# Time mix of a model on one core: the recurrence joined with the output stage, the state's decay on GpSimd, the head statistics on ScalarE by chunk, the bonus during the inversion

## The chip, the cores and the metric

The kernel runs on one core of one Trainium2 chip. Its time is the device time of one execution in microseconds (us). A core has TensorE (matmuls), VectorE, ScalarE, GpSimd (elementwise work) and SyncE, which here only issues loads. In the profile they are PE, with PEld for its weight loads, DVE, ACT, POOL and SP.

## The reference, cut to what matters

The model has two blocks over 256 tokens of width 1024. The second has two layers: feed-forward, mixer, feed-forward. The mixer of the last layer is `rwkv7_time_mix`, with 16 heads of 64. Its end is what the change touches:

```python
def step(state, inp):
    r_t, d_t, k_t, v_t, kk_t, a_t = inp
    sa = einsum('bhij,bhj->bhi', state, -kk_t)
    state = (state * d_t[:, :, None, :] + sa[..., None] * (kk_t * a_t)[:, :, None, :]
             + v_t[..., None] * k_t[:, :, None, :])
    return state, einsum('bhij,bhj->bhi', state, r_t)
_, y = lax.scan(step, zeros, xs)                        # the recurrence
mean = jnp.mean(y, -1, keepdims=True)                   # over the 64 of a head
var = jnp.mean(jnp.square(y - mean), -1, keepdims=True)
y = ((y - mean) * lax.rsqrt(var + RWKV_GN_EPS)).reshape(b, s, d)
y = y * ln_g + ln_b
bonus = jnp.sum(r_ * k_ * r_k, -1, keepdims=True) * v_
y = y + bonus.reshape(b, s, d)
return (y * g) @ w_o                                    # g = sigmoid(xg @ g1) @ g2, g1 1024x160, g2 160x1024
```

## The kernel before, in words

The time mix is four stages, each a block: all engines begin a block together, and the next begins when all are through. They are `rwkv_factors`, `rwkv_inverse`, `rwkv_chunks` and `rwkv_output`; `project_joined` with `w_o` follows, then the feed-forward. Inside a block each engine works through its own list in the order written, and waits on semaphores (`wait_ge`) that others raise (`then_inc`). `link(engine, signal, instruction)` makes the engine wait for the end of its own instruction.

The 256 tokens are 8 chunks of 32 (`N_RC`, `RC`). A tile of y for one chunk is 128 partitions by 256: partition 32q + t is token t of quarter q, and the four quarters hold four heads of 64 each. A matmul of 32 output columns takes one of four column tiles of TensorE's array (`tile_position=(0, 32q)`); a loop over q inside fills the four. The shape of the tile, rows * columns, stands in the profile's rows as 128*32, 32*32, 64*32 or 32*64, and each matmul call in float32 is two records there.

- `rwkv_inverse` makes the 32x32 products of each chunk and head (L3482), inverts the triangles on VectorE (L3571, L3572), makes the values `v` (L3467, copied at L3539), the bonus factors `bon` (L3500) and what the chunks add (`nv`, `kv`). VectorE is through some time before the end of the block, and GpSimd has nothing.
- `rwkv_chunks` goes through the chunks in order. TensorE reads the state S (L3603), VectorE adds (L3646, `W`), TensorE multiplies with the inverse (L3616), VectorE and ScalarE copy one half each (L3652, L3638), TensorE makes the state's update (L3625) and the chunk's y (L3630), VectorE adds them to the decayed state (L3661) and to y (L3655, L3666). The decay of the old state, `Sd = S * cl + kv`, is two VectorE operations of 128x512 (L3648, L3649) in chunks 1 to 6, between L3646 and the copy L3652.
- `rwkv_output` is one pass at full width, 128x2048. VectorE: sum over heads (L3733), mean (L3734), centring (L3735), sum of squares (L3737), reciprocal (L3739), scaling (L3740), gain (L3742), plus bonus and shift (L3744), times the gate (L3746). ScalarE: squares (L3717) and root (L3719). GpSimd: bonus times values (L3724) plus shift (L3727), into `g`. TensorE: the gate g2 in two parts, first all 32 calls with rows 0 to 127 (`ga`, L3704), then all 32 with rows 128 to 159 (`gb`, L3709), each with q inside.
- `project_joined` transposes y (L3195), rounds the weights (L2923) and multiplies (L2898 to L2900).

Weights come through 8 slots of 1 MB. SyncE's `advance` (L401) loads the next unit of a fixed order when the unit in its slot is freed, and its waits stand in that order.

## Time and profile before

| | us |
|---|---|
| time, median of 3 runs | 1957.58 (1957.23 to 1958.78) |
| time of the profiled execution | 1958.1 |
| its span in the trace | 1956.3 |
| inversion to the end, about | 1600 to 1662 |
| recurrence, about | 1662 to 1698.4 |
| output stage, about | 1698.4 to 1719.2 |

Times inside the trace are counted from the start of the span. A row of the order of time is start and duration in us, engine, line, operation, output<-inputs, shapes, how many instructions are merged, and in brackets how long the engine had been idle and what released it. The ends of matmuls are modelled. `PEclk` is the granted clock of TensorE, as a share of 2.4 GHz; 0.50 is 1.2 GHz.

### The profile page before, as it was taken

The page shows a single profiled execution, that of the slowest core. Times are in us where ns is not written, and L with a number is a line of the kernel's source. Part 1 is how long each engine was busy: PE and PEld are TensorE (multiplying, and loading weights), DVE is VectorE, ACT ScalarE, POOL GpSimd, SP SyncE. Part 2 cuts the span into 40 slices and gives each one's busy share as a digit, 9 for nine tenths or more (in the row PEclk, how much of TensorE's full clock was granted, in tenths as well). Part 3 has the DMA queues.
Part 4 walks back from the last instruction along what each step waited for, and adds up shares of the span by engine and source line. Part 5 has one row for each costly group of instructions (what it writes and reads, how often), then busy time and mean ns, then how long its engine had stood idle before and what let it go on. Part 6 is the DMA issues. An engine that isn't in the chain of part 4 may idle for free. (4 is left out here: it accounts for less than half of the span.)

```text
span 1956.3 us, 30051 instructions
## 1 busy us (share of the span) xinstructions
PE 1758.5 (90%) x12670; PEld 1304.8 (67%) x12670; DVE 1105.6 (57%) x1993; ACT 655.7 (34%) x1037; POOL 10.4 (1%) x6
## 2 busy tenths in 40 slices
PE   6898789988988899999987999999998988769998
PEld 5343256763323588888875788878886876558887
DVE  4332254452322777773578677677777372658665
ACT  3111013331100644442243544464444302045443
POOL 0000000000000000000000000000000000200000
PEclk9898889989987999999978999999999989779999
DMA  8999972279999755434211455545542312045540
GB/s 357 415 421 421 421 293 80 93 298 420 421 421 421 296 194 193 162 104 183 105 47 58 157 178 188 183 162 189 180 168 84 131 38 89 4 150 189 182 168 22
DMA packets 58190, 405.27 MB, mean 207 GB/s; under 512 B 6416, under 2 KB 7824, under 8 KB 10432
## 3 DMA queue, kind: packets, MB, share of 16 engines
q1 hardware_dynamic: 58048, 403.25, 53.5%
q8 instruction: 104, 1.70, 0.4%
q14 instruction: 38, 0.31, 0.0%
HBM read 402.18 MB, written 1.05 MB: 206 GB/s over the span
## 5 line engine op out<-in xcount | busy, mean ns | idle before, releaser
L2092 PE MATMUL ps<-ffn_x,ffn_wh 128*128 128x512 f32 x1408 | 496.2, 407 | 10.4 <-DVE ffn_x L2226 7.2
L2095 PE MATMUL ps<-ffn_x,ffn_wl 128*128 128x256 f32 x1408 | 376.6, 281 | 0.0
L2092 PEld LDWEIGHTS ps<-ffn_x,ffn_wh 128*128 128x128 f32 x1408 | 269.6, 192 | 84.1 <-issue 11.0
L2233 DVE TENSOR_TENSOR ffn_wl<-w,ffn_wh 128x2048 fp32r<-128x2048 f32 x132 | 301.4, 2286 | 1.7 <-ACT ffn_wh L2177 0.3
L2095 PEld LDWEIGHTS ps<-ffn_x,ffn_wl 128*128 128x128 f32 x1408 | 258.2, 189 | 1.6
L2177 ACT CAST ffn_wh<-w 128x2048 fp32r<-128x2048 f32 (+1 forms) x140 | 252.9, 1806 | 4.5 <-PEq L715 3.5
L2192 ACT COPY ffn_part_low<-ps 128x512 f32<-128x512 f32 x88 | 51.5, 585 | 338.7 <-PE ps L2095 337.9
L2237 DVE TENSOR_TENSOR ffn_z<-ps,ffn_part_low 128x512 f32<-128x512 f32 x88 | 60.8, 690 | 161.2 <-ACT ffn_part_low L2192 161.0
L2136 PE MATMUL ps<-ffn_wh,ffn_hidh 128*128 128x512 f32 x352 | 138.2, 393 | 0.4 <-issue 0.4
L2138 PE MATMUL ps<-ffn_wh,ffn_hidl 128*128 128x512 f32 x352 | 137.5, 391 | 0.0
L2137 PE MATMUL ps<-ffn_wl,ffn_hidh 128*128 128x512 f32 x352 | 137.3, 390 | 0.0
L1196 DVE TENSOR_TENSOR slot_y<-ps,slot_y 128x512 fp32r<-128x512 f32 x32 | 22.1, 691 | 124.5 <-ACT slot_y L1148 124.5
L1148 ACT CAST slot_y<-ps 128x512 fp32r<-128x512 f32 x32 | 18.7, 586 | 187.6 <-PE ps L1053 187.6
L1236 DVE TENSOR_TENSOR h<-h,ps 128x272 f32<-128x272 f32 x128 | 50.9, 434 | 53.9 <-PE ps L1066 53.8
L1028 PE MATMUL ps<-w,xg 128*32 128x512 f32 x560 | 75.7, 635 | 4.2 <-DMA w<-in_moe_gu 4.2
L2136 PEld LDWEIGHTS ps<-ffn_wh,ffn_hidh 128*128 128x128 f32 x352 | 66.1, 188 | 15.1 <-issue 0.7
L2138 PEld LDWEIGHTS ps<-ffn_wh,ffn_hidl 128*128 128x128 f32 x352 | 66.1, 188 | 14.7
L2137 PEld LDWEIGHTS ps<-ffn_wl,ffn_hidh 128*128 128x128 f32 x352 | 66.1, 188 | 12.7
L1028 PE MATMUL ps<-w_extra,xg 128*32 128x512 f32 x416 | 59.2, 670 | 4.0 <-DMA w_extra<-in_moe_gu 4.0
L2241 DVE TENSOR_TENSOR ffn_z<-ffn_z,rs 128x512 f32<-128x512 f32 x88 | 60.5, 691 | 2.9
L1065 PE MATMUL ps<-spread,slot_y 128*128 128x272 f32 x128 | 46.6, 381 | 12.5 <-DVE h L1236 8.3
L1053 PE MATMUL ps<-w_extra,slot_hidT 128*32 128x512 f32 x256 | 39.8, 732 | 11.8 <-DMA w_extra<-in_moe_dn 10.8
(588 smaller groups left out, 2722.0 us busy)
## 6 DMA issues: line engine op xcount, KB each, us to landing
w<-in_ffn_gu SPq DMA_DIRECT2D x88, 1024.0 KB, 4.8
w<-in_moe_gu SPq DMA_DIRECT2D x70, 1024.0 KB, 18.6
w_extra<-in_moe_gu SPq DMA_DIRECT2D x52, 1024.0 KB, 25.9
w<-in_ffn_dn SPq DMA_DIRECT2D x44, 1024.0 KB, 4.8
w_extra<-in_moe_dn SPq DMA_DIRECT2D x32, 1024.0 KB, 26.2
w<-in_moe_dn SPq DMA_DIRECT2D x26, 1024.0 KB, 26.8
sq<-in_moe_dn SPq DMA_DIRECT2D x6, 1024.0 KB, 27.9
sq<-in_moe_gu SPq DMA_DIRECT2D x6, 1024.0 KB, 26.5
```

What stands on the lines that cost most here:

```text
L1028: mm = nc.tensor.matmul(K.ps[R, i % 2, :], xg[:, i % 2, k, R], w[:, j * 512:(j + 1) * 512], start=k == 0, stop=k == KT - 1, tile_position= ...
L1236: v.tensor_tensor(K.h[:, m], K.h[:, m], K.ps[:, 6 + m % 2, 0:L1], ALU.add).then_inc(added.sem, 1)
L2092: return nc.tensor.matmul(pair_of(b)[:, a], high[:, s, tile(a, k)], X[:, k], start=k == 0, stop=False)
L2095: return nc.tensor.matmul(pair_of(b)[:, a, 0:SEQ], low[:, s, tile(a, k)], XH[:, k], start=False, stop=k == KT - 1)
L2136: nc.tensor.matmul(out, hidh[:, f, tok], high[:, s, w], start=first, stop=False)
L2137: nc.tensor.matmul(out, hidh[:, f, tok], low[:, s, w], start=False, stop=False)
L2138: mm = nc.tensor.matmul(out, hidl[:, f, tok], high[:, s, w], start=False, stop=final)
L2177: nc.scalar.copy(high[:, n % parts, at], S.buf(units[n])[:, at]).then_inc(*w_high.one())
L2192: nc.scalar.copy(part_low[:], pair_of(b)[:, :, SEQ:]).then_inc(*low_copied.one())
L2233: nc.vector.tensor_tensor(low[:, s], S.buf(units[n]), high[:, s], ALU.subtract).then_inc(*w_split.one())
L2237: nc.vector.tensor_tensor(z[:, b % 2], pair_of(b)[:, :, 0:SEQ], part_low[:], ALU.add).then_inc(*added.one())
L2241: nc.vector.tensor_tensor(z[:, b % 2], z[:, b % 2], K.rs[:, 1:2, 0:SEQ].to_broadcast([P, 2, SEQ]), ALU.mult).then_inc(*scaled.one())
```

## The change

`rwkv_output` is gone. Its work goes to three places.

- **Inversion.** GpSimd makes bonus and shift in `g`, as soon as the last values are copied.
- **Recurrence.** GpSimd makes `Sd` in chunks 1 to 6, behind the state's update. VectorE sums the heads of chunk c-1 (`total`) ahead of its copy, and subtracts the mean of chunk c-2 (`centre`) behind it. ScalarE scales the sum to the mean and squares chunk c-1 head by head, with the sum in the accumulator (`spread`).
- **End, in the same block.** `root`, reciprocal, scaling, gain, bonus are done for two halves of four chunks, and the gate multiplies two chunks at a time. TensorE makes the gate after its last chunk by `gate(c)`, in other banks and columns of PSUM.

The core of the diff:

```diff
+ in rwkv_inverse:
+        @block.gpsimd
+        def _(pool):
+            pool.wait_ge(*v_taken.at(N_RC))
+            by = bon[:].rearrange("p c (h a) -> p (c h) a", a=1).to_broadcast([P, 4 * N_RC, HD])
+            link(pool, bonus_made, nc.gpsimd.tensor_tensor(heads(g[:]), heads(v[:]), by, ALU.mult))
+            pool.wait_ge(*S.arrived(unit))
+            nc.gpsimd.tensor_tensor(g[:], g[:], ln[:, 1:2].to_broadcast([P, N_RC, QW]), ALU.add)
+ in rwkv_chunks, SyncE:
+            S_.advance(sp)
+ TensorE:
+            def gate(c):
+                tok = slice(c * RC, (c + 1) * RC)
+                for q in range(4):
+                    R, cols = quad(q), slice(q * QW, (q + 1) * QW)
+                    nc.tensor.matmul(K.ps[R, (c + 4) % 8, QW:2 * QW], low[:, 0, tok], S_.buf(ga)[:, cols], start=True, stop=False, tile_position=(0, q * RC))
+                    mm = nc.tensor.matmul(K.ps[R, (c + 4) % 8, QW:2 * QW], low[0:GATE_LORA - P, 1, tok], S_.buf(gb)[:, cols], start=False, stop=True,
+                                          tile_position=(0, q * RC))
+                if c % 2:
+                    mm.then_inc(*g_made.one())
...
+            pe.wait_ge(*S_.arrived(ga))
+            pe.wait_ge(*S_.arrived(gb))
+            for c in range(N_RC):
+                if c == 4:
+                    pe.wait_ge(*y_done.at(N_RC))
+                gate(c)
+ ScalarE:
+            def spread(c):
+                act.wait_ge(*sum_made.at(c + 1))
+                link(act, K.act_step, nc.scalar.activation(st[:, 1, c], st[:, 0, c], ACT.Copy, scale=-1.0 / HD))
+                for h in range(4):
+                    last = nc.scalar.activation(junk[:], y[:, c, h * HD:(h + 1) * HD], ACT.Square, bias=st[:, 1, c, h], accum_out=st[:, 2, c, h])
+                    if h < 3:
+                        link(act, K.act_step, last)
+                last.then_inc(*spread_made.one())
+            def root(i):
+                act.wait_ge(*spread_made.at(N_RC // 2 * (i + 1)))
+                nc.scalar.activation(st[:, 3, halves[i]], st[:, 2, halves[i]], ACT.Sqrt, bias=K.eps[:, 2:3], scale=1.0 / HD).then_inc(*rooted.one())
             for c in range(N_RC):
                 act.wait_ge(*sa_made.at(2 * c + 2))
                 nc.scalar.copy(SA[:, P:2 * P], K.ps[:, 3, 0:P]).then_inc(*sa_ready_a.one())
+                if c:
+                    if c > 1:
+                        act.wait_ge(*spread_made.at(c - 1))
+                    spread(c - 1)
+            root(0)
+            act.wait_ge(*spread_made.at(N_RC - 1))
+            spread(N_RC - 1)
+            root(1)
+        @block.gpsimd
+        def _(pool):
+            for c in range(1, N_RC - 1):
+                pool.wait_ge(*st_ready.at(c))
+                link(pool, carried, nc.gpsimd.tensor_tensor(Sd[:], S[:], cl[:, :, c:c + 1].to_broadcast([P, KT, HD]), ALU.mult))
+                nc.gpsimd.tensor_tensor(Sd[:], Sd[:], kv[c], ALU.add).then_inc(*carried.one())
+ VectorE:
+            def total(c):
+                dve.wait_ge(*y_done.at(c + 1))
+                vv.reduce_sum(st[:, 0, c], heads(y[:, c]), AX).then_inc(*sum_made.one())
+            def centre(c):
+                dve.wait_ge(*spread_made.at(c + 1))
+                at = heads(y[:, c])
+                vv.tensor_tensor(at, at, st[:, 1, c].to_broadcast([P, 4, HD]), ALU.add).then_inc(*centred.one())
             for c in range(N_RC):
                 if c:
                     dve.wait_ge(*as_made.at(c))
                     vv.tensor_tensor(of_g(W), of_par[:, :, :, 0], of_g(nv[0][:, c]), ALU.add).then_inc(*w_ready.one())
-                    if c < N_RC - 1:
-                        link(dve, K.dve_step, vv.tensor_tensor(Sd[:], S[:], cl[:, :, c:c + 1].to_broadcast([P, KT, HD]), ALU.mult))
-                        vv.tensor_tensor(Sd[:], Sd[:], kv[c], ALU.add).then_inc(*K.dve_step.one())
-                        carried = K.dve_step.now()
+                    total(c - 1)
                 dve.wait_ge(*sa_made.at(2 * c + 1))
                 vv.tensor_copy(SA[:, 0:P], K.ps[:, 2, 0:P]).then_inc(*sa_ready.one())
+                if c > 1:
+                    centre(c - 2)
...
                     if c:
-                        dve.wait_ge(*carried)
+                        dve.wait_ge(*carried.at(2 * c))
...
+            total(N_RC - 1)
+            for i, part in enumerate(halves):
+                n = N_RC // 2
+                dve.wait_ge(*rooted.at(i + 1))
+                link(dve, K.dve_step, vv.reciprocal(st[:, 4, part], st[:, 3, part]))
+                for c in (N_RC - 2, N_RC - 1) if i else ():
+                    centre(c)
+                dve.wait_ge(*centred.at(n * (i + 1)))
+                at = heads(y[:, part].rearrange("p c n -> p (c n)"))
+                by = st[:, 4, part].rearrange("p c h a -> p (c h) a").to_broadcast([P, 4 * n, HD])
+                link(dve, K.dve_step, vv.tensor_tensor(at, at, by, ALU.mult))
+                link(dve, scaled, vv.tensor_tensor(y[:, part], y[:, part], ln[:, 0:1].to_broadcast([P, n, QW]), ALU.mult))
+                link(dve, K.dve_step, vv.tensor_tensor(y[:, part], y[:, part], g[:, part], ALU.add))
+            for p in range(4):
+                dve.wait_ge(*g_made.at(p + 1))
+                pair, banks = slice(2 * p, 2 * p + 2), slice((2 * p + 4) % 8, (2 * p + 4) % 8 + 2)
+                vv.tensor_tensor(y[:, pair], y[:, pair], K.ps[:, banks, QW:2 * QW], ALU.mult)
```

## Rows read from the trace of the kernel before

**Rows 1.** The page, engine totals: busy us, share of the span, instructions.

```profile
PE 1758.5 (90%) x12670; PEld 1304.8 (67%) x12670; DVE 1105.6 (57%) x1993; ACT 655.7 (34%) x1037; POOL 10.4 (1%) x6
```

**Rows 2.** Windows: recurrence, gate products by clock, output stage, projection's start.

```profile
core 0: us, PE busy (x) PEld busy (x) DVE busy (x) ACT busy (x) POOL busy (x), PEclk, DMA share, GB/s
1662.00:1698.40 36.40, 27.54 (x1184) 21.14 (x1184) 23.23 (x49) 2.12 (x8) 0.00 (x0) 0.69 0.02 5
1698.40:1702.60 4.20, 3.77 (x37) 2.02 (x41) 3.85 (x3) 0.00 (x0) 3.71 (x2) 0.51 0.00 0
1702.60:1707.90 5.30, 5.28 (x96) 2.70 (x88) 3.32 (x2) 1.91 (x1) 5.30 (x1) 1.00 0.02 3
1698.40:1719.20 20.80, 9.05 (x128) 4.72 (x128) 17.77 (x9) 2.23 (x2) 10.24 (x2) 0.66 0.18 66
1727.40:1733.10 5.70, 5.64 (x13) 4.46 (x14) 0.01 (x1) 0.06 (x1) 0.00 (x0) 0.50 0.51 185
```

**Rows 3.** Order of time, output stage: start, duration, engine, line, idle before.

```profile
1697.95 0.42 DVE L3666 TENSOR_TENSOR rw_r<-ps,rw_r 128x256 f32<-128x256 f32 x1 [0.54 <-PE ps L3630]
1701.00 1.40 DVE L3734 TENSOR_SCALAR rw_st<-rw_st 128x32 f32<-128x32 f32 x1
1716.74 2.29 DVE L3746 TENSOR_TENSOR rw_r<-rw_r,ps 128x2048 f32<-128x2048 f32 x1
1719.33 3.65 PE L3195 MATMUL ps<-cst,rw_r 128*128 128x128 f32 x16 [11.45 <-PEq L3673]
```

**Rows 4.** Order of time, TensorE: end of the recurrence and both gate products.

```profile
1696.81 1.07 PE L3630 MATMUL ps<-rw_a,rw_sc 32*32 32x64 f32 x32
1698.83 5.47 PE L3704 MATMUL ps<-w,rw_low 128*32 128x256 f32 x64 [0.94 <-PEq L3581]
1704.22 3.65 PE L3709 MATMUL ps<-w,rw_low 32*32 32x256 f32 x64
```

**Rows 5.** Order of time, TensorE: two lines of one shape, then two shapes.

```profile
1606.73 2.47 PE L3493 MATMUL ps<-cst,rw_kk 128*32 128x128 f32 x84
1609.02 0.85 PE L3500 MATMUL ps<-cst,rw_r 128*32 128x2 f32 x77
...
1674.42 0.68 PE L3625 MATMUL ps<-rw_a,rw_bp 32*64 32x64 f32 x32 [0.46 <-DVE rw_a L3652]
1675.03 0.65 PE L3630 MATMUL ps<-rw_a,rw_sc 32*32 32x64 f32 x32
```

**Rows 6.** Full-array matmuls by line; then L3704's durations, ns min/median/max.

```profile
L3267 PE MATMUL ps<-rw_mix,w 128*128 128x256 f32 (+1 forms) x160 | 34.9, 380 | 0.0
...
L3704 PE MATMUL ps<-w,rw_low x64: 379/577/635, 1698.8 to 1703.9; 128*32 128x256 f32 x64
```

**Rows 7.** One chunk in order of time; then L3625 by line.

```profile
1672.41 0.42 DVE L3646 TENSOR_TENSOR rw_a<-ps,xn 128x256 f32<-128x256 f32 x1
1673.64 0.27 ACT L3638 COPY rw_a<-ps 128x128 f32<-128x128 f32 x1 [3.88 <-PE ps L3616]
1674.08 0.28 DVE L3652 COPY rw_a<-ps 128x128 f32<-128x128 f32 x1
1675.24 0.69 DVE L3661 TENSOR_TENSOR rw_sg<-ps,rw_sg 128x512 f32<-128x512 f32 x1 [0.55 <-PE ps L3625]
...
1679.45 0.69 DVE L3661 TENSOR_TENSOR rw_sg<-ps,rw_sg 128x512 f32<-128x512 f32 x1 [0.41 <-PE ps L3625]
...
L3625 PE MATMUL ps<-rw_a,rw_bp 32*64 32x64 f32 x224 | 5.1, 294 | 2.1 <-DVE rw_a L3652 1.4 <-ACT rw_a L3638 0.5 <-issue 0.2
```

**Rows 8.** Order of time, GpSimd.

```profile
1698.74 3.62 POOL L3724 TENSOR_TENSOR rw_g<-rw_v,rw_bonus 128x2048 f32<-128x2048 f32 x1 [1698.30 <-POOLq L3581]
1702.50 6.63 POOL L3727 TENSOR_TENSOR rw_g<-rw_g,w 128x2048 f32<-128x2048 f32 x1
```

**Rows 9.** By line and shape, ScalarE: activation with a bias tile, accumulator read.

```profile
L2736 ACT ACTIVATE nsa_p<-nsa_s,nsa_stat 128x128 f32<-128x128 f32 x16 | 6.4, 402 | 39.9 <-DVE nsa_stat L2848 39.9
...
L2736 ACT ACTIVATION_READ_ACCUMULATOR nsa_p<-nsa_s,nsa_stat 128x1 f32 x32 | 6.0, 186 | 0.0
```

More of the change, by code:

```diff
@@ L3185, in rwkv @@
             kv = [x.rearrange("p (f i) -> p f i", i=HD) for x in kv]
-            rwkv_inverse(K, a, k, r, kk, ar, bp, kp, sc, bon, mix_v, v, kv, tm, nv, flat(sg), flat(K.xn))
+            ln_unit = rwkv_inverse(K, a, k, r, kk, ar, bp, kp, sc, bon, mix_v, v, kv, tm, nv, flat(sg), flat(K.xn), g)
             tm = tm.rearrange("p (t u) -> p u t", t=RC)
-            rwkv_chunks(K, ar, cl, bp, kv, sc, tm, nv, y, flat(a), flat(sg))
-            rwkv_output(K, y, v, low, g, bon, flat(K.xn)[:, 0:2 * D])
+            K.retire("kv_made", "kv_taken", "out_turned")
+            rwkv_chunks(K, ar, cl, bp, kv, sc, tm, nv, y, flat(a), flat(sg), low, g, ln_unit)
         def turn(m):
@@ L3427, in _, with rwkv_inverse @@
             receptance(7)
-def rwkv_inverse(K, bt, kt, rk, kend, ar, bp, kp, sc, bon, mix_v, v, kv, turned, nv, room, room2):
+def rwkv_inverse(K, bt, kt, rk, kend, ar, bp, kp, sc, bon, mix_v, v, kv, turned, nv, room, room2, g):
     nc, S = K.nc, K.stream
@@ L3438, in rwkv_inverse @@
         made, masked, ends_made, ends_taken = K.sig("tile_made"), K.sig("tile_stored"), K.sig("t_made"), K.sig("taken_a")
-        bonus_made, inverted = K.sig("out_made"), K.sig("taken_v")
+        rk_made, inverted = K.sig("out_made"), K.sig("taken_v")
         v_made, v_taken, v_unit = K.sig("lin_made"), K.sig("lin_stored_s"), K.sig("unit_done")
@@ L3445, in rwkv_inverse @@
             S.free(wv[j], v_unit.at(j + 1) if j < 3 else v_made.at(N_RC))
+        unit, bonus_made = S.take("ln_rows"), K.sig("scaled")
+        ln = S.buf(unit).rearrange("p (j n) -> p j n", j=2)
+        heads = lambda ap: ap.rearrange("p c (h d) -> p (c h) d", d=HD)
         tok = lambda c: slice(c * RC, (c + 1) * RC)
@@ L3501, in _ @@
                                           tile_position=(0, f % 4 * RC))
-            mm.then_inc(*bonus_made.one())
+            mm.then_inc(*rk_made.one())
             pe.wait_ge(*ends_taken.at(8))
@@ L3534, in _ @@
                 nc.scalar.copy((bp, kp)[n // 4][:, 2 * (n % 4):2 * (n % 4) + 2], K.ps[:, n].rearrange("p (s n) -> p s n", s=2)).then_inc(*ends_taken.one())
-            act.wait_ge(*bonus_made.at(1))
+            act.wait_ge(*rk_made.at(1))
             nc.scalar.copy(bon[:], K.ps[:, 0, 0:4 * N_RC].rearrange("p (c h) -> p c h", c=N_RC))
@@ L3574, in _, with rwkv_chunks @@
             vv.transpose(square(turned), T[:]).then_inc(*inverted.one())
-def rwkv_chunks(K, ar, cl, bp, kv, sc, tm, nv, y, room, room2):
-    nc = K.nc
-    with ExitStack() as ctx:
+        @block.gpsimd
[5 more added lines that the diff above has]
+            nc.gpsimd.tensor_tensor(g[:], g[:], ln[:, 1:2].to_broadcast([P, N_RC, QW]), ALU.add)
+    return unit
+def rwkv_chunks(K, ar, cl, bp, kv, sc, tm, nv, y, room, room2, low, g, unit):
+    nc, S_ = K.nc, K.stream
+    with ExitStack() as ctx:
+        st = ctx.enter_context(nc.sbuf_tensor("rw_st", [P, 5, N_RC, 4, 1], F32))
+        junk = ctx.enter_context(nc.sbuf_tensor("rw_junk", [P, HD], F32))
+        y_done, sum_made, spread_made, rooted = K.sig("y_done"), K.sig("exp_asked"), K.sig("exp_done"), K.sig("gated")
+        centred = K.sig("centred")
+        carried, scaled, g_made = K.sig("carried"), K.sig("scaled"), K.sig("lin_made")
+        ga, gb = S_.take("c_g2a"), S_.take("c_g2b")
+        S_.free(unit, scaled.at(2))
+        S_.free(ga, g_made.at(4))
+        S_.free(gb, g_made.at(4))
+        ln = S_.buf(unit).rearrange("p (j n) -> p j n", j=2)
+        heads = lambda ap: ap.rearrange("p (h d) -> p h d", d=HD)
+        halves = [slice(0, N_RC // 2), slice(N_RC // 2, N_RC)]
         S, Sd = (room2[:, j * KT * HD:(j + 1) * KT * HD].rearrange("p (f i) -> p f i", i=HD) for j in range(2))
@@ L3593, in rwkv_chunks, with _ @@
         block = ctx.enter_context(nc.Block())
+        @block.sync
+        def _(sp):
+            S_.advance(sp)
         @block.tensor
         def _(pe):
+            def gate(c):
[7 more added lines that the diff above has]
+                    mm.then_inc(*g_made.one())
             def read_state(c, j):
@@ new lines, in _ @@
+                vv.tensor_tensor(y[:, c].rearrange("p (a n) -> p a n", a=2), half, (y if c else nv[1])[:, c].rearrange("p (a n) -> p a n", a=2),
+                                 ALU.add).then_inc(*y_done.one())
+            total(N_RC - 1)
[11 more added lines that the diff above has]
+                link(dve, K.dve_step, vv.tensor_tensor(y[:, part], y[:, part], g[:, part], ALU.add))
```

73 lines of the change are left out of this document (removed).

## The prediction

> **What bounds the kernel now.** I read the page first: TensorE is busy 90% of the span [rows 1]. That average says nothing of the stage that is changed, so I went on to the windows around it. In the output stage, 20.8 us long, TensorE is busy 9.05 us, VectorE 17.77 and GpSimd 10.24 [rows 2]: VectorE's row of full-width operations ends this stage. The order of instructions in time shows it: the last operation of the recurrence (L3666) starts at 1697.95 and takes 0.42, so it ends at T = 1698.37; VectorE then runs through head statistics, scale and shift up to L3746, which ends at 1716.74 + 2.29 = 1719.03, and TensorE's transposes for the projection start at 1719.33 [rows 3]. The tail is thus 1719.03 - 1698.37 = 20.66 us, all on VectorE's clock. The low-rank gate products of TensorE are done by 1704.22 + 3.65 = 1707.87 [rows 4], 11 us before they are needed. In the recurrence the chain goes round between TensorE and VectorE, with a period near 4.4 us.
>
> **The gate products.** This is the largest term, and the diff names it only in passing. Before, all 32 products with `ga` run first (four column tiles q after each other), then all 32 with `gb`. The new `gate(c)` puts the `gb` product of a q straight behind its `ga` product. The first has tiles of 128*32, the second of 32*32 [rows 4], so TensorE now changes its tile shape at each of the 64 calls, where it changed once.
> A call is two records (32 calls, x64 records) [rows 4]. What hides their length today is that the four column tiles work side by side: 64 records of 256 columns take 3.65 us, 0.057 each, while at full array, one record after the other in one place, 160 records take 34.9 us, 0.218 each [rows 4, 6]. So one tile by itself needs 0.218 per record, and four together give a fourth of it.
> What happens at a change of shape? In a chunk of the recurrence L3625 (32*64) runs from 1674.42 for 0.68, to 1675.10; L3630 (32*32) waits for nothing new, and starts at 1675.03, 0.07 before that modelled end [rows 5]. From L3704 to L3709 it is 1698.83 + 5.47 = 1704.30 against 1704.22: 0.08 [rows 4]. All of the some 25 changes of shape without a wait in the inversion and the recurrence that I looked at have this 0.07. Where the line changes and the shape doesn't (L3493 to L3500), the next starts 0.18 before the end of the last (1606.73 + 2.47 = 1609.20 against 1609.02) [rows 5]. I read it so: a matmul of a new shape starts only when those of the old shape are through the array, on whichever column tile they are. Four tiles side by side are then no longer possible inside a call, nor across calls.
> The Trainium skill (TensorEngine Tiling (Array Packing), section Tiling Modes, Key Properties) has both sides: tiles work independently and in parallel, and changing the tiling mode drains TensorE. By the first sentence alone this edit would cost nothing; by the second, all 64 calls run one at a time. It gives no time for the drain; the rows above do, and they agree with the second.
> Price of a call: its first record holds the place for 0.218, its second lasts 0.379 less the 0.07 [rows 6]: 0.218 + 0.379 - 0.07 = 0.527 us at full clock. At half clock 0.218 doubles to 0.436, and a record lasts 0.635 [rows 6]: 0.436 + 0.635 - 0.07 = 1.00 us. Bounds of the whole, 64 calls: 33.7 us and 64.0 us, against 9.04 now (1698.83 to 1707.87).
> Which clock? Before, the granted clock was 0.51 from 1698.4 to 1702.6 and 1.00 from there to the end of the gate products [rows 2]; TensorE had been working on and off in the recurrence before, and without a break from 1698.8. I keep that pattern: the gate products now start right behind the last L3630 (1696.81 + 1.07 - 0.07 = 1697.81 [rows 4]), run 4.8 us at 1.2 GHz (4.8 calls), and the other 59.2 calls take 31.2 us at 2.4 GHz: end 1733.8 (1697.81 + 4.8 + 31.2). The products stream for most of each call, so I expect the clock to stay.
> VectorE's last multiplication waits for the last pair: 0.14 from TensorE's end to VectorE's start (1675.10 to 1675.24 [rows 5, 7]), then 0.69 for its 128x512 [rows 7]. The output stage ends at 1734.6 instead of 1719.03: **+15.6 us**.
>
> **The rest of the output stage** hides under this. Without the gate products VectorE would go from T like this (128x1024 on the straight line between 0.69 at 512 and 2.29 at 2048, so 1.22 [rows 3, 7]): ScalarE, behind its last copy, still has the squares of chunk 6 (2.5 us by the terms below, from 1696.65, so to T + 0.8), then a root of 0.3; VectorE's first half of three passes runs from about T + 1.5 to T + 5.3; a small reciprocal and two centrings 1.1, three passes with their links 3.8: T + 10.2; four gate multiplications 2.5: T + 12.7 instead of T + 20.66. That 8.0 us is what the rewrite takes from VectorE, and none of it reaches the end while TensorE is busy to T + 35.4. By that same cover (over 20 us) errors in the statistics cost nothing. If the cover is gone the stage ends at T + 12.7, which is the first rival.
> Bonus and shift on GpSimd go to the inversion: 3.62 + 6.63 = 10.2 us [rows 8] from about 1639 on, when the last values are copied and VectorE has finished its inversion. They end by 1650, before the recurrence begins at 1662. They were hidden before too (end 1709.13 [rows 8], while VectorE had the statistics): 0. The block boundary that goes is inside T + 12.7.
>
> **The recurrence.** Two 128x512 operations (L3648, L3649) leave VectorE in six chunks, at 0.69 as L3661 [rows 7]. They delay its half of the copy: L3652 starts 1.67 after L3646 (1672.41 to 1674.08) though ScalarE's half is there at +1.23, done at +1.50 [rows 7]. What it holds up is TensorE's L3625, and its idle time on that copy is 1.4 us in all chunks together [rows 7]. So the gain is at most 1.4 us, of TensorE time, not the 12 x 0.69 of VectorE.
> What comes in on VectorE: `total` (256 wide, 0.42 as L3646 [rows 7]) between L3646 and the copy, over by +0.8; `centre` (0.42) behind the copy, where VectorE waits for TensorE anyway (0.55 idle before L3661 [rows 7]). ScalarE: a head is an ACTIVATE of 64 with a bias tile, under the 0.402 of 128 wide, plus 0.186 for the accumulator [rows 9], plus 0.04: below 0.63. Four and a small copy make 2.5 to 2.75, with the 0.27 of its own copy 3.0 of a period of 4.4. The waits of the links stand in front of the next chunk's copy, with over 1 us to spare: 0.
> GpSimd gets the decay, 512 wide: 0.90 each at the rate of L3724 and 1.66 each at that of L3727 [rows 8], so 1.8 to 3.3, with three handoffs of 0.14 2.2 to 3.75 us, behind L3661 and ahead of the next L3661. That distance is 1679.45 - 1675.93 = 3.5 us today [rows 7]. I take one of each rate, 3.0: just in time. VectorE's next L3661 then waits for `carried`, with L3666 and, on TensorE, the next read of the state behind it. Both ends: -1.4 us, and 6 x 0.5 - 1.4 = +1.6 if GpSimd is slow. I take **-1.0**.
> For a two-input add of 2048 the Trainium skill (GPSIMD Engine Reference, section Performance versus the Vector engine) has 4497 ns alone, and says that the port is shared with VectorE operations of two SBUF inputs or in a two-port mode. The trace agrees: L3727 took 6.63 beside such operations, and a 32-wide TENSOR_SCALAR took 1.40 until L3724 ended (1702.36) [rows 3, 8]. With the page's figure a fourth of the add would be an estimated 1.1, and the sum the same. No operation of the second kind stands in the new loop.
>
> **Moved loads.** SyncE is released by the scale (now about T + 9) and then by the last gate product; the loads behind it (L401) are weights of the next feed-forward. Two of them now start near 1734, with the whole projection still in front of their use: 0.
>
> **After the stage.** TensorE was idle from 1707.87 to 1719.33, and the projection's first 5.7 us ran at a granted clock of 0.50 [rows 2, 3]. TensorE will now be busy to the end of the stage, with breaks left behind the transposes. Going to full clock would give up to 5.7/2 = 2.9 us; the other end is 0. I take **-1.3**.
> Sum: +15.6 - 1.0 - 1.3 = +13.3 us on the profiled execution (1958.1 us, span 1956.3), which is 0.5 over the median of 1957.58: forecast **1971 us**.
>
> **Rivals.**
> 1. Shapes share the array: the changes cost nothing beyond today's 9 us. Then the gate products are done by T + 9 at the latest, VectorE's chain ends the stage, T + 12.7: -8.0 - 1.0 - 1 = 1947.5 us. It decides below some 12.5 us of TensorE time for the gate. For it: the four-fold overlap in rows 4. Against: the 0.07. And even without a drain two calls on one column tile stand behind each other: 64 x 2 x 0.218 = 27.9 us if TensorE issues strictly in order, +9 and still slower. Neighbouring tiles overlapping by half would be 14 us, 1951. Chance 0.10 for all that is faster.
> 2. The clock. If one tile at a time doesn't hold 2.4 GHz, the gate products take 64 us: end 1761.8 + 0.8, +43.6 for this term: 2000 us. The recurrence, with TensorE busy 27.5 of 36.4 us, had 0.69; the gate products without a break had 1.00 [rows 2]. Half and half would be 64/(0.5/0.527 + 0.5/1.00) = 44 us, 1979. Chance of worse than half and half 0.05.
> 3. GpSimd late in each chunk: +2.6 over my value, inside the main range and without another sign.
>
> **Numbers.** Forecast case 0.83 (range 1964 to 1984: all at full clock with -1.4 and -2.9, up to half and half with +1.6 and no gain behind), rival 1 0.10, rival 2 0.05, no visible change 0.02. The range 1964 to 1984 leaves out the rivals and some tail. A change of 0.2%, 3.9 us, is about what can be told from none. Faster 0.10, same 0.02, slower 0.88.
>
> **What would show it.** Right: in the new trace the gate's matmuls span 33 to 45 us with 128*32 and 32*32 in turn, VectorE stands idle some 20 us before its last one to three multiplications with TensorE as what it waits for, and the transposes start near 1734. L3625's idle time on VectorE's copy is near 0, GpSimd's two operations take 2.2 to 3.8 us. Wrong: gate products in about 9 us and transposes near 1710. If the chunk period grows over 4.4 us the GpSimd term had the wrong sign.

## The result and the profile after

| | before | changed |
|---|---|---|
| time, median of 5 runs, us | 1957.58 (1954.45 to 1960.27) | 1972.31 (1969.97 to 2001.62) |
| time of the profiled execution | 1958.1 | 1972.31 |
| its span | 1956.3 | 1970.5 |

The changed kernel is slower: ratio 1.0105, 95% interval 1.0073 to 1.0137. Its five executions were 1969.97, 1970.28, 1972.31, 1997.34 and 2001.62; the ratio leaves out the highest as disturbed and still holds the other high one. The two high ones are no accident, as the last experiment shows; the three low ones alone (median 1970.28) are 0.65% over before.

The order of time on TensorE, at the end of the recurrence and the end of the gate products:

```profile
1697.75 0.65 PE L3667 MATMUL ps<-rw_a,rw_sc 32*32 32x64 f32 x32
1698.33 0.62 PE L3630 MATMUL ps<-w,rw_low 128*32 128x256 f32 x2
1698.88 0.61 PE L3631 MATMUL ps<-w,rw_low 32*32 32x256 f32 x2
1699.42 0.62 PE L3630 MATMUL ps<-w,rw_low 128*32 128x256 f32 x2
...
1732.77 0.61 PE L3631 MATMUL ps<-w,rw_low 32*32 32x256 f32 x2
1734.67 1.94 PE L3195 MATMUL ps<-cst,rw_r 128*128 128x128 f32 x16 [1.29 <-PEq L3593]
```

This answers to [rows 4]. The two blocks of 64 records, 32 calls each, have become 64 pieces of 2 records, in turn 128*32 and 32*32, and each begins 0.545 us after the last (1699.42 less 1698.33 is 1.09 for two). From 1698.33 to 1732.77 + 0.61 = 1733.38 they fill 35.05 us instead of 9.04. By line, then the waits on VectorE in that stretch (line, what it waited for, us in total, times, longest), then VectorE's order of time (leaving out what lies between):

```profile
L3630 PE MATMUL ps<-w,rw_low 128*32 128x256 f32 x64 | 19.8, 391 | 0.0
L3631 PE MATMUL ps<-w,rw_low 32*32 32x256 f32 x64 | 19.6, 386 | 0.0
```
```profile
DVE rw_r L3763 <- PE ps L3631: 22.6, 3, 8.1
```
```profile
1698.46 0.42 DVE L3745 TENSOR_TENSOR rw_r<-ps,rw_r 128x256 f32<-128x256 f32 x1 [0.20 <-PE ps L3667]
...
1707.50 1.22 DVE L3759 TENSOR_TENSOR rw_r<-rw_r,rw_g 128x1024 f32<-128x1024 f32 x1
1708.76 0.69 DVE L3763 TENSOR_TENSOR rw_r<-rw_r,ps 128x512 f32<-128x512 f32 x1
1715.93 0.69 DVE L3763 TENSOR_TENSOR rw_r<-rw_r,ps 128x512 f32<-128x512 f32 x1 [6.49 <-PE ps L3631]
1724.68 0.69 DVE L3763 TENSOR_TENSOR rw_r<-rw_r,ps 128x512 f32<-128x512 f32 x1 [8.06 <-PE ps L3631]
1733.43 0.69 DVE L3763 TENSOR_TENSOR rw_r<-rw_r,ps 128x512 f32<-128x512 f32 x1 [8.06 <-PE ps L3631]
```

VectorE's own work is over at 1708.72 (1707.50 + 1.22), 9.8 us behind the recurrence's end (T = 1698.46 + 0.42 = 1698.88), and it then stands idle 22.6 us for TensorE. The stage ends at 1733.43 + 0.69 = 1734.12, against 1719.03 before: +15.1, of which 14.6 lie behind T (35.24 us instead of 20.66) and 0.5 ahead of it. Windows by the granted clock, the recurrence and then the gate:

```profile
core 0: us, PE busy (x) PEld busy (x) DVE busy (x) ACT busy (x) POOL busy (x), PEclk, DMA share, GB/s
1662.50:1698.90 36.40, 28.85 (x1187) 21.93 (x1187) 20.80 (x50) 14.55 (x68) 13.97 (x12) 0.64 0.02 5
1698.90:1734.20 35.30, 34.49 (x127) 8.47 (x126) 11.78 (x15) 3.04 (x15) 0.00 (x0) 1.00 0.09 30
```

The whole gate ran at 2.4 GHz. One chunk of GpSimd's new work, and by line what the recurrence's TensorE step waits for, the counterpart of the last row of [rows 7]:

```profile
1676.46 1.06 POOL L3708 TENSOR_TENSOR rw_sg<-rw_sg,rw_cl 128x512 f32<-128x512 f32 x1 [2.21 <-DVE rw_sg L3740]
1677.60 1.27 POOL L3709 TENSOR_TENSOR rw_sg<-rw_sg,rw_k 128x512 f32<-128x512 f32 x1
```
```profile
L3662 PE MATMUL ps<-rw_a,rw_bp 32*64 32x64 f32 x224 | 5.1, 301 | 0.6 <-ACT rw_a L3694 0.5
```

### The profile page after: what moved, and what is told of

Same layout as the page of the kernel before. It is cut to its first block and busy times, and to the rows that moved or that the text cites. A ratio compares the mean times of both kernels' runs of the same rounds, so it can differ in the third digit from the quotient of the medians.

```text
span 1970.5 us, 30140 instructions
## 1 busy us (share of the span) xinstructions
PE 1781.1 (90%) x12670; PEld 1305.8 (66%) x12670; DVE 1097.3 (56%) x2000; ACT 669.4 (34%) x1109; POOL 22.3 (1%) x18
## 5 line engine op out<-in xcount | busy, mean ns | idle before, releaser
L2136 PEld LDWEIGHTS ps<-ffn_wh,ffn_hidh 128*128 128x128 f32 x352 | 66.1, 188 | 15.1 <-issue 0.7
L2137 PEld LDWEIGHTS ps<-ffn_wl,ffn_hidh 128*128 128x128 f32 x352 | 66.1, 188 | 12.7
L1065 PE MATMUL ps<-spread,slot_y 128*128 128x272 f32 x128 | 45.6, 374 | 12.4 <-DVE h L1236 8.8
```

Of the source, the lines that this page charges most:

```text
L2136: nc.tensor.matmul(out, hidh[:, f, tok], high[:, s, w], start=first, stop=False)
L2137: nc.tensor.matmul(out, hidh[:, f, tok], low[:, s, w], start=False, stop=False)
```

## The experiments

Medians are in us. The kernels of one group below ran on one chip and share its runs of the kernel before: median 1957.09 (23 runs) for the first four, 1961.38 (12) for the next four, 1959.7 (20) for the three after these, 1961.36 (11) for the last.

### The order of the gate's calls

**Changed kernel, shape changed 16 times (by chunk).**

```diff
+                for part in "ab":
+                    for q in range(4):
+                        mm = gate_part(part, c, q)     # "a": the ga product, "b": the gb product
```

> The changed kernel with one edit: in each chunk the four calls with ga (128*32) come first, then the four with gb (32*32); 16 changes of tile shape instead of 64. Theory A (a change of shape empties the array): a group of four calls on four column tiles costs what one call costs now, 0.547 us, so the gate takes about 16 x 0.55 = 8.8 us at full clock, up to 16 at half; VectorE's chain, whose last pass ended at 1708.7, then sets the end at about 1711.5 instead of 1734.1: 22.6 us less, 1950 us, and some 8 us under the kernel before. Theory B (a call stands behind another one on its own column tile, the shape does not matter): also fast, about 9 us for the gate. Theory C (the added waits of ScalarE and GpSimd make the change slow): no gain, 1970.

Measured: 1955.18 (1946.42 to 1958.52, 10 runs), ratio 0.998 [0.9962, 0.9998].

The order of time on TensorE:

```profile
1700.20 0.64 PE L3630 MATMUL ps<-w,rw_low 128*32 128x256 f32 x8
1700.77 0.63 PE L3631 MATMUL ps<-w,rw_low 32*32 32x256 f32 x8
...
1707.57 0.63 PE L3631 MATMUL ps<-w,rw_low 32*32 32x256 f32 x8
```

Four calls of one shape on the four column tiles take 0.57, nearly what a single call takes when the shape changes behind it (0.545). The gate's products are through in 9.4 us (1698.77 to 1708.20), VectorE waits for none of them, and the stage ends at T + 11.9. With 16 changes of shape instead of 64, and nothing else undone, the slowdown is gone. Why this kernel's median lies 3.9 us over that of the next one, which the expectation puts within 0.5 us of it, the profiles don't show: the next one's stage is 0.5 us longer.

**Shape changed 3 times (by half).**

```diff
+                for part in "ab":
+                    for c in range(first, first + 4):  # first = 0, then 4
+                        for q in range(4):
+                            mm = gate_part(part, c, q)
```

> The changed kernel with the gate in the order of the kernel before, by halves: all ga calls of chunks 0 to 3, then all gb calls, the same for 4 to 7; 3 changes of shape. Theory A: gate 7.0 us at full clock, which nobody waits for, since VectorE's chain ends the stage in both: same time as the by-chunk order within 0.5 us, about 1949 to 1950. Theory C: 1970.

Measured: 1951.32 (1946.59 to 1955.21, 12 runs), ratio 0.9962 [0.9946, 0.9977]: faster than before, by 0.38%. In the order of time, TensorE and then VectorE:

```profile
1701.52 1.93 PE L3630 MATMUL ps<-w,rw_low 128*32 128x256 f32 x32
1703.39 1.93 PE L3631 MATMUL ps<-w,rw_low 32*32 32x256 f32 x32
```
```profile
1701.65 0.42 DVE L3747 TENSOR_TENSOR rw_r<-ps,rw_r 128x256 f32<-128x256 f32 x1 [0.25 <-PE ps L3664]
...
1711.96 2.48 DVE L3765 TENSOR_TENSOR rw_r<-rw_r,ps 128x512 f32<-128x512 f32 x4
```

The gate is over in 7.5 us, and VectorE ends the stage, at 1714.44, which is T + 12.37 (T = 1702.07).

**Same three changes, four calls in a row on one column tile.** The loop over q stands outside that over c.

> The changed kernel with only 3 changes of shape, but four calls in a row on the same column tile (q outside, chunk inside). Theory A says that shape is what costs and nothing of a wait for the own column tile; if neighbours overlap only where the next call is on another tile, the gate's 64 calls take 64 x 2 x 0.218 = 27.9 us less the overlap at each change of q, end of the stage near 1726 and time near 1963. If each column tile had a deep queue of its own: 7 to 9 us, time 1950. Theory B (own tile is the cause, not the shape): as slow as the changed kernel or nearly, 28 to 35 us for the gate.

Measured, one run: 1952.6.

The order of time on TensorE:

```profile
1699.88 4.59 PE L3631 MATMUL ps<-w,rw_low 32*32 32x256 f32 x32
1704.40 4.59 PE L3630 MATMUL ps<-w,rw_low 128*32 128x256 f32 x32
```

16 calls take 4.52 us from start to start, 0.28 each, against 0.117 with q inside (1.87 for 16) and 0.545 with a change of shape at each. So a column tile that follows itself is a cost of its own, but under that of a change, and less than two records in strict order (2 x 0.218). The gate now ends the stage, at T + 19.2 instead of T + 12.4; the one total, 1952.6, doesn't show these 7 us, since its recurrence began 7.5 us earlier than in the profile of the kernel by half (1659.19 against 1666.67). The clock in the recurrence's last microsecond and then under these calls:

```profile
1694.00:1695.00 1.00, 1.00 (x40) 0.83 (x32) 0.42 (x1) 0.94 (x5) 0.00 (x0) 0.50 0.00 0
1695.80:1699.80 4.00, 4.00 (x31) 2.14 (x29) 3.89 (x5) 2.49 (x12) 0.00 (x0) 1.00 0.00 0
```

A stream of calls on one column tile, without changes of shape, thus came up from 1.2 to 2.4 GHz.

**Shape changed at 59 of the 63 steps, successive calls on different column tiles.** Behind the `ga` product of one q comes the `gb` product of the q before; at the start and the end of each half two calls of one shape meet (the expectation counts 62 changes).

```diff
+                gate_part("a", *calls[0])
+                for n, (c, q) in enumerate(calls):
+                    if n + 1 < len(calls):
+                        gate_part("a", *calls[n + 1])
+                    mm = gate_part("b", c, q)
```

> The changed kernel with the gb call of each q behind the ga call of the next q: consecutive calls are always on different column tiles, and the shape still changes at 62 of 63 steps. Theory A: 0.547 us a call as now, 35 us for the gate at full clock, 1971 us. Theory B: calls on different tiles overlap, 9 to 14 us, 1950 us.

Measured, one run: 2002.49.

The order of time, and the window of the gate:

```profile
1703.37 1.07 PE L3630 MATMUL ps<-w,rw_low 128*32 128x256 f32 x4
1704.37 1.06 PE L3631 MATMUL ps<-w,rw_low 32*32 32x256 f32 x2
1705.36 1.06 PE L3630 MATMUL ps<-w,rw_low 128*32 128x256 f32 x2
```
```profile
1703.37:1762.85 59.48, 59.48 (x132) 10.79 (x128) 11.53 (x15) 3.23 (x15) 0.00 (x0) 0.50 0.06 18
```

Two neighbours now never stand on one tile, and they still run one at a time, while the first two calls, of one shape (x4), take 1.00 together: what costs is the change of shape, not the tile. But each call takes 0.99 and not 0.545: the gate took 59.5 us, TensorE was busy in all of them, and the granted clock was 0.50 from the first call to the last. That is rival 2 of the prediction, and the next runs go after it.

### Which clock the gate gets

**The kernel before, with only the order of the gate's calls changed.** The `gb` call moves into the loop behind the `ga` call of the same q; nothing else differs from before.

> The kernel before with one part of the change alone: the gb call of each q stands behind its ga call (64 changes of shape instead of 1). Theory A: the gate's products take 35 us at full clock, 64 at half; they start at 1698.8 and end at 1734 or at 1763; VectorE's last multiplication, 2.29 us over the full width, waits for them: the stage ends at 1736 (or 1765) instead of 1719.0: 1975 us, or 2003 to 2004 in executions with the gate at half clock. That would be all of the change's loss. Theory C (the loss lies in the added waits): no change, 1957.

Measured: 2005.61 (2001.41 to 2010.16, 4 runs), ratio 1.0222 [1.0197, 1.0247].

The gate's first call, its window, and VectorE's last operation of the stage:

```profile
1705.53 1.03 PE L3704 MATMUL ps<-w,rw_low 128*32 128x256 f32 x2 [1.00 <-PEq L3581]
```
```profile
1705.53:1768.95 63.42, 63.40 (x128) 11.44 (x128) 15.29 (x8) 2.23 (x2) 10.07 (x2) 0.50 0.05 17
```
```profile
1769.03 2.29 DVE L3742 TENSOR_TENSOR rw_r<-rw_r,ps 128x2048 f32<-128x2048 f32 x1 [45.68 <-PE ps L3705]
```

The order alone makes the old kernel slower, by more than the whole change does in its low executions, since here the gate begins at 1.2 GHz and stays there for 63.4 us. Before, the dense order also began at 0.51, and came to 1.00 some 4 us into the gate [rows 2]. All four executions here are over 2001 us, where the changed kernel has low ones too. That the 1.0 us of the block boundary makes the difference is not shown: in this profile the clock was at 0.50 in the last 5.5 us ahead of the gate already.

**The changed kernel with a dense gate ahead.** The gate is computed twice, first in the dense order, then in that of the change.

```diff
+                for part, (kk, buf, n) in enumerate(((0, ga, P), (1, gb, GATE_LORA - P))):
+                    for c in range(first, first + 4):
+                        for q in range(4):
+                            nc.tensor.matmul(... tile_position=(0, q * RC))
             for c in range(N_RC):
                 gate(c)
```

> The changed kernel; ahead of its gate TensorE makes the same products once more in the dense order (all ga calls of four chunks, then all gb calls, four column tiles side by side), and the gate in its own order overwrites them, so the output is the same. Theory D (the one-tile stream keeps the clock that it is entered with: full in the changed kernel's profiled execution, half in that of e4_other_tile): the dense part takes 7 to 11 us and brings the clock to 1.0, the gate follows at 0.547 us a call, 35 us, in every execution; time 1971 + 8 = 1979 us, all executions within 6 us. Theory E (the clock in the gate is chance, whatever comes before): some executions at 1979, some 28 us later.

Measured: 1983.12 (1978.74 to 1984.39, 4 runs), ratio 1.011 [1.0086, 1.0135].

The order of time on TensorE:

```profile
1699.60 7.52 PE L3679 MATMUL ps<-w,rw_low 128*32 128x256 f32 x128
1707.05 0.62 PE L3630 MATMUL ps<-w,rw_low 128*32 128x256 f32 x2
```

All executions are near 1982, 21.7 over before: the 14.2 of the changed kernel at full clock and the 7.5 of the dense gate. None lies where 64 calls at half clock would have put it, 28.5 higher. In the profiled execution the clock was at 1.00 before the dense gate began, so that it brings the clock up is inferred from the four totals, and four are few.

**The changed kernel with a pause ahead of the gate.**

```diff
+            pe.wait_ge(*scaled.at(2))
             for c in range(N_RC):
```

> The changed kernel with one wait ahead of the gate: TensorE stands idle until VectorE has done its second pass with the gain, about 9 us after the last chunk. Theory D: the gate is entered at half clock and stays there, 64 calls of 1.00 us; the stage ends at about 1707.5 + 64 + 0.8 = 1772 instead of 1734: 2009 us, in every execution. Theory E, or a clock that rises in the course of a long busy stretch: 9 + 35 + a few us, 1980 to 1985 us.

Measured: 2012.34 (2009.11 to 2018.24, 4 runs), ratio 1.0258 [1.0233, 1.0283].

The gate's first call and its window:

```profile
1715.40 1.03 PE L3630 MATMUL ps<-w,rw_low 128*32 128x256 f32 x2 [8.73 <-DVE rw_r L3759]
```
```profile
1715.40:1778.80 63.40, 63.40 (x128) 11.46 (x128) 3.18 (x4) 0.00 (x0) 0.00 (x0) 0.50 0.05 17
```

After 8.7 idle us it began at 1.2 GHz and did not rise in 63.4 us. The clock was at 0.50 in the last microseconds of the recurrence too, so this profile doesn't show the pause bringing it down; what speaks for it is that all four executions are over 2009 us.

### The other edits

**By half, with the decay back on VectorE** (two operations of 128x512 in six chunks, as before; GpSimd's are taken out).

> The fast version (gate by halves) with one part of the change undone: the decay of the state is back on VectorE, between the first addition and the copy; GpSimd has nothing in the recurrence. My prediction gave the move 1.0 us, at most 1.4; the changed kernel's trace shows none from the first copy to the end of the recurrence (35.6 us in both). With the total of the heads also in that place VectorE's half of the copy would start at about +2.0 instead of +1.2 after L3646, 0.5 to 0.8 us later than needed, in six chunks: 2 to 5 us slower than the fast version, 1953 to 1956. If the decay hides as before: same time, 1951.

Measured: 1951.57 (1946.78 to 1954.35, 7 runs), ratio 0.9954 [0.9937, 0.9971]. With the decay on GpSimd it was 0.9962 [0.9946, 0.9977]: no difference. TensorE's idle time on VectorE's copy is back, 1.0 us in all, and nothing is seen of it in the time; the expected loss of 2 to 5 us did not come.

**By half, with bonus and shift at the recurrence's end**, on GpSimd behind its last decay.

> The gate order of the by-half kernel, with the bonus product and the shift (the two GpSimd passes of 2048) moved from the inversion to behind the last state decay of the recurrence. Everything is computed. Theory (the move of the bonus was worth nothing in the changed kernel only because the gate covered it; with the short gate it is worth up to 4 us): GpSimd is free near 6 us before T, the end of the recurrence. The two passes need 3.6 + 4.5 to 6.6 us, so they end 2 to 5 us after T, and VectorE's first bonus add is due near T + 3.8: 0 to 1.5 us of wait, and up to 1 us more if the passes slow VectorE's own operations in the recurrence. 1951.3 to 1954, ratio 0.996 to 0.998. Rival (the passes beside the recurrence slow its VectorE operations much more, since each chunk has operations with two inputs in memory): over 1955. Rival (hidden entirely): as the by-half kernel, 1951, ratio 0.996; in the trace no wait of the bonus add on GpSimd.

Measured: 1953.29 (1948.6 to 1957.53, 10 runs), ratio 0.9965 [0.9951, 0.9978]. The order of time on GpSimd, then on VectorE:

```profile
1701.30 4.62 POOL L3709 TENSOR_TENSOR rw_g<-rw_g,w 128x2048 f32<-128x2048 f32 x1
```
```profile
1703.86 3.15 DVE L3758 TENSOR_TENSOR rw_r<-rw_r,rw_st 128x1024 f32<-128x1024 f32 x1
1707.05 1.23 DVE L3759 TENSOR_TENSOR rw_r<-rw_r,w 128x1024 f32<-128x1024 f32 x1
```

The bonus isn't waited for (GpSimd is through at 1705.92, the bonus add stands behind L3759). What it costs is another thing: VectorE's first scaling, 1.22 in the other kernels, takes 3.15 and ends 1.09 after GpSimd's add does (1707.01 against 1705.92): of the 2.06 us in which the two ran together VectorE got by these numbers some 0.1 us of work done. The stage ends at T + 14.3 instead of T + 12.4. The cost, 1.9 us, is in the trace; the two ratios don't tell it from nothing.

**By half, decay on VectorE, GpSimd finishing chunks 0 to 5.** GpSimd scales, gains and adds the bonus for a chunk at a time while the recurrence goes on, with roots and reciprocals by chunk; VectorE does this for the last two chunks only.

```diff
+            for c in range(by_pool):                   # by_pool = 6
+                pool.wait_ge(*recip_made.at(c + 1))
+                pool.wait_ge(*centred.at(c + 1))
+                at = heads(y[:, c])
+                link(pool, posted, nc.gpsimd.tensor_tensor(at, at, st[:, 4, c].to_broadcast([P, 4, HD]), ALU.mult))
+                link(pool, posted, nc.gpsimd.tensor_tensor(y[:, c], y[:, c], ln[:, 0], ALU.mult))
+                nc.gpsimd.tensor_tensor(y[:, c], y[:, c], g[:, c], ALU.add).then_inc(*posted.one())
```

> From the kernel with by-half gate and the decay on VectorE: GpSimd, which then has nothing to do in the recurrence, does the scale, gain and bonus passes of chunks 0 to 5 chunk by chunk during the recurrence (18 passes of 512, 1.1 to 1.7 us each: 3.3 to 5.1 us per chunk of 4.4); roots are taken by chunk. VectorE finishes chunks 6 and 7 alone. Everything is computed. Theory (VectorE's chain behind T ends the stage in the by-half kernel, at about T + 12.7, and its passes are the price): it loses nine passes' worth (three over six chunks, some 5.5 us) and gains eight small operations, so the stage ends near T + 8: 4 us off, 1947.5, ratio 0.993 to 0.994. Rival (GpSimd's share of the port slows VectorE in the recurrence: 18 passes beside VectorE's): the chunk period grows by 0.3 us or more, 2 us over all, and the total is as before this edit, 1951, ratio 0.995 to 0.996. Rival (GpSimd late): 5.1 us per chunk, chunk 5 ends near T + 4; VectorE's last chunks wait for it, stage ends near T + 11.

The kernel it starts from, once more on the same chip:

> The kernel with by-half gate and the decay on VectorE once more, unchanged, on the same chip as the one with GpSimd finishing chunks 0 to 5, so that the two can be compared directly: 1951.5, ratio 0.9954 as before. Theory on the finishing passes: this one is 4 us above the other. Rival: the two are equal within 1.5 us.

Measured: 1947.87 (1942.33 to 1957.0, 7 runs), ratio 0.9941 [0.9919, 0.9964], against 1952.48 (1949.63 to 1954.6, 8 runs), ratio 0.9961 [0.9945, 0.9976], for the other. By line on GpSimd, then VectorE's order of time:

```profile
L3711 POOL TENSOR_TENSOR rw_r<-rw_r,w 128x256 f32<-128x256 f32 x6 | 4.4, 728 | 0.5
L3710 POOL TENSOR_TENSOR rw_r<-rw_r,rw_st 128x256 f32<-128x256 f32 x6 | 3.7, 614 | 40.8 <-DVE rw_st L3729 40.8
```
```profile
1699.86 0.42 DVE L3764 TENSOR_TENSOR rw_r<-ps,rw_r 128x256 f32<-128x256 f32 x1 [0.54 <-PE ps L3665]
...
1707.70 1.28 DVE L3736 TENSOR_TENSOR rw_r<-rw_r,ps 128x512 f32<-128x512 f32 x2
```

The stage ends at T + 8.7 (1708.98 less 1700.28), against T + 11.9 in the kernel it starts from (1715.43 less 1703.57). The recurrence took 37.35 us against 37.08, at a granted clock of 0.55 in both, so GpSimd's 18 operations cost VectorE's chain little there. The expectation had the size of an operation wrong (256 wide, 0.61 and 0.73 each, not 512), so GpSimd had more room than thought. This is the fastest kernel of the study, 0.6% under before; over its own starting point the medians are 4.6 us apart, the trace shows 3.2, and the intervals overlap.

### The changed kernel once more

> The changed kernel once more, unchanged, for more executions of it. Theory (the one-tile-at-a-time stream of gate products keeps whichever clock level it is entered with, and in this kernel it is entered from a recurrence whose granted clock goes up and down): the executions fall into two groups with next to nothing between, some near 1970 to 1975 and some near 1997 to 2005, 28.5 us apart as 64 calls of 0.547 us and of 1.00 us are. Rival (the clock rises somewhere inside the gate): times spread evenly between the groups, 1975 to 1995.

Measured, 6 runs: 1973.52, 1973.77, 2003.57, 2005.29, 2008.02, 2008.98, median 2004.43; no ratio, since they are no one group. With the five of the first measurement, 5 of 11 executions lie within 1970.0 to 1973.8 and 6 within 1997.3 to 2009.0, and none between: the two groups that were expected. Windows of the profiled run here (1973.52), two ahead of the gate and one in it; below, the one just ahead of the gate in the run with different tiles in a row (2002.49):

```profile
1691.00:1693.00 2.00, 1.86 (x88) 1.38 (x72) 1.29 (x4) 1.29 (x6) 0.76 (x1) 0.58 0.03 8
1697.00:1699.60 2.60, 1.97 (x116) 1.45 (x96) 1.77 (x5) 1.05 (x5) 0.00 (x0) 1.00 0.00 0
1699.60:1734.60 35.00, 35.00 (x136) 8.63 (x128) 11.56 (x16) 3.45 (x17) 0.00 (x0) 1.00 0.09 31
```
```profile
1701.00:1703.37 2.37, 2.37 (x96) 1.86 (x88) 1.07 (x4) 1.38 (x7) 0.00 (x0) 0.50 0.03 7
```

The recurrence in front is the same code; in one the clock had come up some 6 us before the gate, in the other it was down, and the gate kept it. What decides this, the runs don't show. No profile fell on an execution of the changed kernel itself near 2000, so that its gate was at 1.2 GHz there is inferred: from the distance of the groups (means 28.6 us apart in the first measurement and 32.8 in the second; 64 calls at 0.99 instead of 0.545 are 28.5, and the 4 us over that in the second stay open), from the mean clock over the span (0.910 to 0.918, against 0.927 to 0.933), and from the profiles with other tiles in a row, with the gate's order alone and with the pause, all of whose totals are over 2001 us. An estimate agrees with the clocks: 35 us at 1.00 turned into 64 at 0.50 would take the mean from 0.931 to 0.916.

## Why the prediction was right, and where it wasn't

Forecast 1971 (1964 to 1984), measured 1972.31. On the profiled execution: +13.3 forecast, +14.2 measured. (The terms named for the low end of the range, 33.7 us of gate with -1.4 and -2.9, give 1966.6 and not 1964.)

**The gate products: the mechanism held.** The 0.07 at a change of shape [rows 5] was indeed a drain. Run by run: without the changes 7.5 us, with 64 of them 35; whether neighbours share a column tile makes no difference. A call was priced at 0.527 and took 0.545 at full clock; at half, 1.00 and 0.99. That is 0.11 more than two records in strict order (2 x 0.218 [rows 6]); what this rest is made of, no run separates. Forecast for the gate's span 36.0, measured 35.05: the call was 1.2 us too cheap in all, and the 4.8 us at half clock that were put first (2.3 us) did not come, since the clock was up at the start. The rule of the Trainium skill (TensorEngine Tiling (Array Packing), section Tiling Modes) that a change of mode drains TensorE agrees with these runs.

**The clock: the step that failed.** "I keep that pattern: ... 4.8 us at 1.2 GHz ..., and the other ... at 2.4 GHz" took it that TensorE's clock rises under this stream as it did under the dense one. It doesn't: in three kernels the gate began at 0.50 and was there to its end, 59.5 to 63.4 us later, with TensorE busy all along. An execution costs some +13 or some +43, and what settles it, as far as the profiles go, is the clock when the recurrence ends. There it goes up and down, in the profiled execution of the changed kernel like this:

```profile
1692.00:1694.00 2.00, 2.00 (x96) 1.66 (x88) 1.05 (x3) 1.06 (x5) 0.38 (x1) 0.50 0.01 4
1696.00:1698.00 2.00, 1.40 (x81) 1.20 (x85) 1.54 (x5) 0.62 (x3) 0.00 (x0) 1.00 0.00 0
```

So the forecast holds for one of two outcomes. That the first median fell there (3 executions of 5) is luck: in the second measurement 4 of 6 are in the other group, and the median, 2004.43, lies outside the stated range. Rival 2, with its 2000 us well priced, was far too low at 0.05: it came in 6 of 11 executions. Its time was derived right, its condition only in part: one tile at a time with changes of shape does hold 2.4 GHz once it is there (35 us), but doesn't come up to it. What was missed is that [rows 2] hold no stretch in which such a stream began at half clock, so that nothing bore out the rise.

**The rest of the output stage hides: right.** VectorE alone was forecast to T + 12.7; with the gate out of the way (by half) it ended at T + 12.4. So the rewrite itself took 8.3 us from the stage (20.66 to 12.4), as forecast (8.0), and the median fell by 5.8 (1951.32 against 1957.09); with the gate's order of the change the stage went to 35.24 us, +14.6.

**Recurrence: -1.0 forecast, nothing to be seen in its length.** From the start of VectorE's first copy to T it was 35.57 before and 35.62 after:

```profile
1662.80:1698.37 35.57, 26.84 (x1168) 20.40 (x1159) 23.23 (x49) 2.12 (x8) 0.00 (x0) 0.69 0.02 5
1663.26:1698.88 35.62, 28.12 (x1170) 21.17 (x1162) 20.79 (x50) 14.53 (x68) 13.97 (x12) 0.64 0.02 5
```

The idle time on the copy fell from 1.4 to 0 as forecast; GpSimd took 1.06 + 1.27, from start to end 2.41 with the handoff between them (3.0 with handoffs was the forecast) and was never late. TensorE's idle time as a whole fell by 1.2 us (8.73 to 7.50), and its busy time grew by 1.3 at a lower granted clock, 0.64 instead of 0.69. The clock in the recurrence is what the forecast left out, and it goes with more than the edit was to bring: the old code took 35.57 us with TensorE busy 26.84 at 0.69, and 37.77 with 29.12 at 0.59 (the kernel with only the gate's order changed). The changed recurrence took 34.8 us at 0.71 (two profiles), 35.6 at 0.64, and 35.4 to 37.8, mean 36.6, at 0.59 or 0.60 (six). That leaves room for the forecast gain and doesn't show it; and with the decay back on VectorE the total is the same.

**Bonus in the inversion, moved loads: 0, right** for this kernel: GpSimd's two operations took 3.62 and 4.50 us and were over at 1647.49. With the short gate the bonus's place is worth at most the 1.9 us by which VectorE's scaling is slower beside GpSimd's add. The Trainium skill (GPSIMD Engine Reference, section Key points) says that GpSimd shares its SBUF interfaces with VectorE operations of two SBUF inputs; the 3.15 against 1.22 agrees.

**After the stage: -1.3 forecast, -0.9 measured** (14.2 less the 15.1 of the stage's end), and -1.0 in the second profile of the changed kernel. But from the stage's end to the end of the span all 14 profiles lie between 236.0 and 237.8 us, so a term of this size is not told from what comes anyway. The transposes, 1.94 instead of 3.65 [rows 3], gained nothing, as the projection waits for VectorE's L2944 behind them. What came is that the first stretch of the projection at half clock shrank:

```profile
1742.80:1746.50 3.70, 3.69 (x9) 2.92 (x10) 0.00 (x0) 0.00 (x0) 0.00 (x0) 0.50 0.86 294
```

9 matmuls of it instead of 13 [rows 2], at 0.2 us each.

**Rival 1** (the changes cost nothing) fell as a statement on shapes, but its time, 1947.5, is that of the kernel without them to within 4 us: 1951.32.

## What to carry to other kernels

Moving a loop's body into a helper can turn an order "all of one shape, then all of the other" into "one of each in turn"; on tiles that work side by side this costs the whole overlap, here 64 x 0.545 us against 7.5, and more than the rewrite around it saved (+0.6% to +0.7% in one group of executions and +2.1% to +2.3% in the other, against -0.38% with 3 changes of shape). Look at the record counts in the order of time: x64 in one piece against x2. And take a price that depends on the clock at both levels, with a chance for each, when the stretch in front leaves the clock now up, now down.

## What the runs showed of the hardware that was not expected

- A stream of single 32-column tiles with a change of shape at each call kept the clock that it began with, both ways: 35 us at 2.4 GHz in three profiled runs (the changed kernel twice, and the one with the dense gate ahead), and 59.5, 63.4 and 63.4 us at 1.2 GHz in three others, with TensorE busy in all of them. The Trainium skill (TensorE: Matmul & The Clock Gate, section What's actually happening) has it that activity releases the throttle; if activity is the busy time of the profile, these runs speak against it. A dense order began at 0.51 and rose [rows 2], and so did calls on one column tile without changes of shape (0.50, then 1.00 within a microsecond).
- Four calls on the four column tiles take 0.57 us between changes of shape, one alone 0.545. Without a change they take 0.47 (4 x 0.117), so a change costs some 0.1 us beside the lost overlap.
- Calls that follow each other on one tile without a change of shape take 0.28 each, half of a call alone.
- The changed recurrence took 34.8 us at a mean granted clock of 0.71 (two profiles) and 35.4 to 37.8 at 0.59 or 0.60 (six).
- The recurrence's first VectorE copy started between 1659.2 and 1670.2 us in the profiled runs, with next to the same code ahead of it, so one execution's total tells little under 10 us; a stage is to be measured from its own start.
